# Row factors of the softmax through DRAM into the merge stage, unscaled groups prepared first, normalisation on ScalarE, in a decoder layer of three mixers

## What is computed

```python
def one_block(args):                       # fox_attention, 128 queries of all 8 heads
    scores = jnp.einsum('bqhd,bkhd->bhqk', qi, k) * scale
    logits = jnp.where(mask[None, None], scores + bias, -jnp.inf)
    p = jax.nn.softmax(logits, axis=-1)
    return jnp.einsum('bhqk,bkhd->bqhd', p, v)
...
y_b = fox_attention(...) * jax.nn.silu(gbf)
merged = (gates[:, :, 0] * (y_a @ w_up_a) + gates[:, :, 1] * (y_b @ w_up_b)
          + gates[:, :, 2] * (y_c @ w_up_c))
out = merged @ w_out
return layer_norm(ALPHA * x + out, ln_g, ln_b)
```

## Time and profile before

| | us |
|---|---|
| median of 3 runs | 1954.6 (1950.67 to 1956.67) |
| profiled execution, its own time | 1956.44 |
| its span | 1954.8 |
| PE busy | 1916.7 |
| PEld busy | 1625.1 |
| DVE busy | 1125.0 |
| ACT busy | 708.7 |
| POOL busy | 435.1 |

### The profile page before, as it was taken

One profiled execution on the slowest core, in us unless ns is written; L12 is line 12 of the kernel. 1 busy time (PEld: TensorE's weight loads), 2 busy tenths in 40 slices (PEclk: granted clock), 3 DMA queues, 4 the chain that ended last, 5 costly groups with the idle time before them and its releaser, 6 DMA issues. The chain is left out here.

```text
span 1954.8 us, 30551 instructions
## 1 busy us (share of the span) xinstructions
PE 1916.7 (98%) x10560; PEld 1625.1 (83%) x10560; DVE 1125.0 (58%) x2142; ACT 708.7 (36%) x1090; POOL 435.1 (22%) x548
## 2 busy tenths in 40 slices
PE   7999999999999999999999999999999989999998
PEld 6878887888886888888888788888888878999997
DVE  4563235654244655646556665565655568777676
ACT  3121113021033554555555655455555541111110
POOL 1927940498000000000000000000000002222322
PEclk9999999999999999999999999999999989999999
DMA  6224225322432142241513515133142286555542
GB/s 187 65 91 117 89 86 193 66 97 109 138 120 87 56 124 68 66 125 48 138 54 89 186 50 139 54 89 109 48 136 66 87 262 208 167 174 170 174 118 87
DMA packets 105592, 221.69 MB, mean 113 GB/s; under 512 B 11000, under 2 KB 56744, under 8 KB 101928
## 3 DMA queue, kind: packets, MB, share of 16 engines
q1 hardware_dynamic: 92912, 165.61, 26.8%
q0 software_dynamic: 12608, 55.19, 10.2%
HBM read 155.09 MB, written 65.08 MB: 113 GB/s over the span
## 5 line engine op out<-in xcount | busy, mean ns | idle before, releaser
L1447 PE MATMUL g_ps<-x_hi,w_lo 128*128 128x512 f32 x768 | 309.7, 403 | 0.0
L1447 PE MATMUL g_ps<-x_hi,w_hi 128*128 128x512 f32 x768 | 308.2, 401 | 0.0
L1361 DVE TENSOR_TENSOR pt_lo<-t_ps,pt_hi 128x512 fp32r<-128x512 f32 (+2 forms) x320 | 191.7, 607 | 134.3 <-ACT pt_hi L1269 132.9
L1447 PE MATMUL g_ps<-x_lo,w_hi 128*128 128x512 f32 x768 | 228.1, 412 | 3.7 <-PEq L1484 2.7
L697 PE MATMUL tile_ps<-x_hi,w_hi 128*128 128x512 f32 x736 | 228.4, 391 | 1.5 <-DVE w_lo L379 1.5
L697 PE MATMUL tile_ps<-x_lo,w_hi 128*128 128x512 f32 x736 | 226.7, 389 | 0.0
L697 PE MATMUL tile_ps<-x_hi,w_lo 128*128 128x512 f32 x736 | 226.6, 389 | 0.0
L1269 ACT ACTIVATE pt_hi<-t_ps 128x512 fp32r<-128x512 f32 (+2 forms) x320 | 170.4, 534 | 135.0 <-PE t_ps L1406 130.6
L1177 POOL DMA_DIRECT2D mixT<-y_out x63 | 33.8, 536 | 749.4 <-DVE y_out L1315 749.4
L1301 DVE CUSTOM_DVE_ANT_0 s_sb<-s_ps,f_row 128x512 f32<-128x512 f32 (+2 forms) x320 | 180.7, 605 | 19.5 <-PE s_ps L1395 18.8
L1406 PE MATMUL t_ps<-ident,s_sb 128*128 128x128 f32 x1088 | 171.7, 273 | 1.6 <-DVE pt_lo L1361 1.0
(11 more groups left out here) (294 smaller groups left out, 3576.4 us busy)
## 6 DMA issues: line engine op xcount, KB each, us to landing
w_lo_raw<-in_w_tiles SPq DMA_DIRECT2D x96, 512.0 KB, 3.6
gateT<-g_out SPq DMA_DIRECT2D x96, 256.0 KB, 3.0
gate<-gateT SPq DMA_DIRECT2D x64, 384.0 KB, 4.5
qkvT<-zout SPq DMA_DIRECT2D x24, 512.0 KB, 3.2
x_lo_raw<-in_xT SPq DMA_DIRECT2D x20, 512.0 KB, 8.5
silT<-zout SPq DMA_DIRECT2D x16, 512.0 KB, 2.6
k_ll<-qkvT POOLq DMA_DIRECT2D x16, 512.0 KB, 7.4
q_st<-qkvT POOLq DMA_DIRECT2D x16, 512.0 KB, 9.1
```

What stands on the lines that cost most here:

```text
L1361: dve.tensor_tensor(pt_lo[part], t_ps[n % 2][:, 0:keys].rearrange("p (k q) -> p k q", q=P), pt_hi[part].bitcast(F32), ALU.subtract).then_i ...
L1447: mm = pe.matmul(g_ps[c][:], w[j % 2][:, k, :], x[:, k, c * BANK:(c + 1) * BANK], start=(r == 0), stop=(r == 3 * KT - 1))
```

## The change

Attention no longer divides. `y_out` is stored unscaled to `mixT`. The reciprocals of all 16 tiles are taken at once at the head's last tile, PE transposes them in one 16-column matmul into 16 rows of 128 queries, DVE copies these to `inv_row`, and POOL stores them to a new DRAM scratch `inv` of 128 rows (`store_inv`). The last head does this twice: after its first tiles (two rows are wanted early) and at its end, where SP stores the other 14 rows.

In the merge, SP loads the factors of a block with two DMAs (`load_inv`), each broadcasting rows of four heads to 64 partitions, into the part of `y_lo` that belongs to groups 1 and 2. That is free once the block before has lifted its last step, so SP waits for `lifted` in step d = 6. DVE multiplies `sil` of groups 1 and 2 by the factors (`scale`) ahead of `mix *= sil`. From the second block on, groups 0 and 3 (unscaled) are prepared first, and PE waits for all four groups before the block's first matmul instead of for one after another. For the first block the order of the groups stays.

The normalisation `(x - mean) * rstd` of 128x1024 moves from DVE to ACT as one activation with scale `rstd` and bias `-mean * rstd`; DVE computes the bias in one more small operation. The tail after the last block is as before.

```diff
-            def output(at, p):
+            def output(at, p, last):
                 dve.wait_ge(o_low_ready, at(8, p + 1))
-                dve.wait_ge(y_free, at(8, p + 1))
-                dve.tensor_tensor(y[:], o_ps[0:HD, 0, :], o_low[:], ALU.add).then_inc(o_sum, 1)
-                dve.wait_ge(o_sum, at(8, p + 1))
-                dve.tensor_tensor(y[:], y[:], o_ps[0:HD, 1, :], ALU.mult).then_inc(y_ready, 1)
+                dve.wait_ge(y_free, at(9, p + (2 if last and p >= 3 else 1)))
+                dve.tensor_tensor(y_out[p % 2], o_ps[0:HD, 0, :], o_low[:], ALU.add).then_inc(y_ready, 1)
...
+                if p == 7 or (last and p == 0):
+                    dve.tensor_copy(inv_row, o_ps[0:Q_TILES, 1, 0:P]).then_inc(y_ready, 1)
...
-                    if t % 2 == 1:
+                    if t == Q_TILES - 1 or (last and t == 1):
                         dve.wait_ge(p_ready, at(Q_TILES, t + 1))
-                        dve.reciprocal(row_inv[:, t - 1:t + 1], row_sum[:, t - 1:t + 1]).then_inc(inv_ready, 1)
+                        dve.reciprocal(row_inv[:, 0:t + 1], row_sum[:, 0:t + 1]).then_inc(inv_ready, 1)
...
-                pe.wait_ge(inv_ready, at(8, p + 1))
-                for a in range(2):
-                    last = pe.transpose(o_ps[0:HD, 1, a * P:(a + 1) * P],
-                                        row_inv[:, 2 * p + a:2 * p + a + 1].broadcast_to([P, HD]), ident[:])
-                last.then_inc(o_full, 1)
+                if p == 7 or (final and p == 0):
+                    pe.wait_ge(inv_ready, at(1, 2 if final and p else 1))
+                    mm = pe.transpose(o_ps[0:Q_TILES, 1, 0:P], row_inv[:, 0:Q_TILES], ident[:])
+                mm.then_inc(o_full, 1)
...
+            sp.wait_ge(y_ready, HEADS * 9 + 1)
+            sp.dma_start(scr["inv"][(HEADS - 1) * Q_TILES + 2:], inv_row[2:]).then_inc(last_y_stored, 16)
...
+def load_inv(eng, kept, scr, b):
+    rows = scr["inv"].rearrange("(h t) q -> h (t q)", t=Q_TILES)
+    for odd in range(2):
+        eng.dma_start(kept.y_lo[odd * HD:(odd + 1) * HD, 2:6].bitcast(F32),
+                      rows[odd::2, bass.ds(b * BLOCK, BLOCK)].partition_broadcast(HD)).then_inc(kept.mix_loaded[1], 16)
...
+    def scale(g):
+        dve.wait_ge(kept.mix_loaded[1], b * 64 + 64)
...
+        dve.tensor_tensor(kept.sil[g][:], kept.sil[g][:], group(kept.y_lo, g).bitcast(F32),
+                          ALU.mult).then_inc(kept.scaled, 1)
...
                 for d in range(KT):
+                    if d == KT - 2 and not last:
+                        sp.wait_ge(lifted, b * KT + KT)
+                        load_inv(sp, kept, scr, b + 1)
                     sp.wait_ge(m_split, b * KT + (d + 1))
...
+            def normalise(b, m):
+                act.wait_ge(h_rstd, b * 10 + (5 * m + 5))
+                act.activation(x_t[m][:], x_t[m][:], ACT.Identity, scale=rstd[m][:], bias=fix[m][:]).then_inc(h_norm, 1)
...
-                return dve.tensor_scalar(x_t[m][:], x_t[m][:], mean_var[m][:, 0:1], rstd[m][:], ALU.subtract, ALU.mult)
+                dve.tensor_scalar(t, mean_var[m][:, 0:1], r, -1.0, ALU.mult, ALU.mult).then_inc(h_rstd, 1)
...
-                            if d == 0 and k % (KT // YG) == 0:
-                                pe.wait_ge(y_split, b * YG + (k // (KT // YG) + 1))
+                            if d == 0 and k % (KT // YG) == 0 and (first or k == 0):
+                                pe.wait_ge(y_split, b * YG + (k // (KT // YG) + 1 if first else YG))
```

More of the change, by code:

```diff
@@ L1045, in stage_attend @@
         g_bias = sb("g_bias", [P, T_GATE])
-        g_out, y_out = kept.g_out, kept.y_out
+        g_out, y_out = kept.g_out, [y[0:HD] for y in kept.y_out]
+        inv_row = kept.y_out[0][HD:HD + Q_TILES, 0:P]
         k_hh = sb("k_hh", [P, S], F32R)
@@ L1371, in body @@
                                           kept.wu_hi[:, KT - 1 - i].bitcast(F32), ALU.subtract).then_inc(kept.wu_split, 1)
[L1372 removed]
+                    split_y(dve, kept, 0, True)
                 else:
                     split_kq(at(1, 2))
[L1375 removed]
+                output(at, 7, last)
                 for j in splits("tail", last):
@@ L1506, in group, with split_y, product @@
     return t[:, g * (KT // YG):(g + 1) * (KT // YG)]
-def split_y(dve, kept, b):
+def load_inv(eng, kept, scr, b):
[3 more added lines that the diff above has]
+                      rows[odd::2, bass.ds(b * BLOCK, BLOCK)].partition_broadcast(HD)).then_inc(kept.mix_loaded[1], 16)
+Y_ORDER = (0, 3, 1, 2)
+def split_y(dve, kept, b, first=False):
+    order = range(YG) if first else Y_ORDER
+    def scale(g):
+        dve.wait_ge(kept.mix_loaded[1], b * 64 + 64)
+        if g != 1:
+            dve.wait_ge(kept.mix_loaded[g], b * 32 + 32)
+        dve.tensor_tensor(kept.sil[g][:], kept.sil[g][:], group(kept.y_lo, g).bitcast(F32),
+                          ALU.mult).then_inc(kept.scaled, 1)
+    def product(g):
+        if g in (1, 2):
+            dve.wait_ge(kept.scaled, b * 2 + g)
+        else:
+            dve.wait_ge(kept.mix_loaded[g], b * 32 + 32)
+        dve.tensor_tensor(kept.mix[g][:], kept.mix[g][:], kept.sil[g][:], ALU.mult).then_inc(kept.prod, 1)
     def finish(g):
-        dve.wait_ge(kept.y_high, b * YG + (g + 1))
+        dve.wait_ge(kept.y_high, b * YG + (order.index(g) + 1))
         dve.tensor_tensor(group(kept.y_lo, g), kept.mix[g][:], group(kept.y_hi, g).bitcast(F32),
                           ALU.subtract).then_inc(kept.y_split, 1)
-    for g in range(YG):
-        dve.wait_ge(kept.mix_loaded[g], b * 32 + 32)
-        dve.tensor_tensor(kept.mix[g][:], kept.mix[g][:], kept.sil[g][:], ALU.mult).then_inc(kept.prod, 1)
-        if g:
-            finish(g - 1)
-    finish(YG - 1)
+    if first:
+        product(0)
+        scale(1)
+        scale(2)
+        finish(0)
+        product(1)
+        product(2)
+        finish(1)
+        product(3)
+        finish(2)
+        finish(3)
+    else:
+        product(0)
+        product(3)
+        finish(0)
+        finish(3)
+        scale(1)
+        scale(2)
+        product(1)
+        product(2)
+        finish(1)
+        finish(2)
 def stage_merge(nc, io, scr, kept, out):
@@ L1638, in high_y @@
             def high_y(b):
-                for g in range(YG):
-                    act.wait_ge(prod, b * YG + (g + 1))
+                for n, g in enumerate(Y_ORDER):
+                    act.wait_ge(prod, b * YG + (n + 1))
                     act.activation(group(y_hi, g), mix[g][:], ACT.Copy).then_inc(y_high, 1)
@@ L1650, in body @@
                         root(b - 1, 1)
+                    if not first and d == 5:
+                        normalise(b - 1, 1)
                     act.wait_ge(merged, b * KT + (d + 1))
```

93 lines of the change are left out of this document (53 added, 40 removed).

## The result

The changed kernel takes 1958.2 us (median of 20 runs, 1952.7 to 1963.3) where the kernel before took 1952.6 (20 runs): ratio 1.0023, 95% interval 1.0016 to 1.0030. It is slower by about 0.23% (4.5 us; the medians differ by 5.6), which lies just inside the 0.3% that I took for what can be told from no change; with 20 runs each the interval excludes no change. Forecast: 1946.5, 8.1 us less than before. Its profiled execution took 1959.4 us, span 1957.8 (before 1956.4 and 1954.8).

The account below looks back on a forecast made before the run. TensorE, busy 1916.7 of 1954.8 us, was taken as the bound nearly everywhere. Attention -13.1, its end +0.8, second merge block +4.2 and steady blocks 0 sum to -8.1, so 1946.5 us; range 1941.5 to 1951.

Parts of the forecast that it names:

- Steady blocks, "0 us": Six later merge boundaries: y ready 9.4 us early now, over 8 after the change, so no cost.
- Factors arrive late: Rival, steady merge blocks: late factors stop TensorE at every boundary, 23 us in all, time 1970; chance 0.05.
- ScalarE's activation of 128x1024 lies in its idle time: Steady merge blocks: the normalisation moved to ScalarE is covered there, part of the 0 us.
- Second block, +4.2: Merge, block 1: later landing (1.3), nine operations behind it, TensorE's wait and slow clock; +4.2 us, ends +0.8 to +6.8.
- Attention, -13.1 +0.8 = -12.3: Attention and its end: 119 of 128 factor transposes removed give -13.1 us; later stores at the barrier add 0.8.
- a factor transpose is worth less than its starts say: Rival, attention: removed transposes worth 0.088 us each, so -10.4 instead of -13.1, time 1949.2; chance 0.06.
- attention gives less: Rival, attention: another engine's latency paces some tiles, half of the 13.1 us turns into waits, time 1953.0; chance 0.12.
- VectorE's answer comes earlier by more: Attention, after a pair's values: without the multiplication (0.34 us) VectorE's pt_lo comes earlier by more than TensorE's 0.22.
- End of attention, +0.8: Barrier before the merge: two more products and a second store delay SP and the merge by 0.8 us, ends 0.5 and 1.5.
- Normalisation on ScalarE, at nothing: Merge: VectorE hands 0.81 us of normalisation to ScalarE and gains one small operation; counted as no cost.
- The signs of being wrong: Heads not 1.4 to 1.9 us shorter, idle time at a steady boundary, or block 1's wait under 3 or over 8 us.

Follow-up runs that it names:

- own_rows: The changed kernel with the merge's factor loads of blocks 1 to 7 reading rows of silT instead, same number, size and place; ratio 0.9990 to the kernel before, median 1950.1 us.
- copies8: The change with factors stored 8 times, last store after block 0's fourth gate load, natural group order, normalisation on VectorE; ratio 0.9978 to the kernel before.
- no_loads: The changed kernel without the factor loads of blocks 1 to 7, every other instruction kept; ratio 0.9980 to the kernel before, median 1949.2 us.

## Why the prediction was wrong, point by point

No one term explains the miss. The trace is 11.2 us above the sum's -8.1: attention with its end 5.2, the second block 3.3, the steady blocks 3.7 and the last one 0.4, less 1.4 ahead of the heads. In the steady blocks the mechanism was wrong; elsewhere sizes were.

- **Steady blocks, "0 us": the step that failed.** "VectorE has y ready 9.4 us early" and "the factor loads go out at `lifted` 8 and are wanted some 9 us on" left the landing unpriced; a sil load's 8.8 us would have fitted. The second load took 10.1 to 10.7, and VectorE wanted it 5 us after the first was issued (1750.99 to 1755.99). 37.8 us of VectorE's waits came of it, and 3.7 us on TensorE. own_rows shows the source as the cause: with other rows, the same loads leave 44.6 in every block.
- **The rival that came true, in part.** "Factors arrive late" was given 0.05 and a threshold of 18 us from issue to landing, since only the wait for `y` was costed. That wait never stopped TensorE in steady blocks. What stopped it was the second `gate`, behind two adds that GpSimd's late operations stretched, and that at 10.9 to 11.6 us from the first issue to the last landing (0.3 to 1.3 us a block), while 7.5 to 8.4 (own_rows) and 8.7 to 10.1 (copies8) cost nothing. I had asked who waits for `y`, and not which other engines work later because VectorE waits, and what they then meet. "ScalarE's activation of 128x1024 lies in its idle time" is of the same kind: true of ScalarE, but GpSimd starts when it ends. How much of the 3.7 us the normalisation's new place has was not tested; own_rows and no_loads have it there and lose nothing. The path through GpSimd is read from the traces; no run moved GpSimd's operations alone.
- **Second block, +4.2, measured +7.5.** The mechanism was right: nine operations in 5.8 us, a wait of 5.8 forecast and 7.8 found, clock at 0.50 behind it, no wait at step 2. The term mis-sized is the delay of the last landing: 1.3 by bytes over 355 GB/s, 3.1 measured, above its upper bound of 2.6. own_rows returns 3.9 us of block 0 (no_loads 2.9). The longer wait is 2.0 of the 3.3 us that the forecast lacked. The other 1.3 are in block 1, which gained 0.2 instead of the 1.6 that the sum gave it: its old wait of 1.8 is gone, but the slow stretch costs 2.5 (5 us at 0.50) where the sum had 2.0, and there is a new wait of 0.8 us for the second `gate`, whose adds again meet GpSimd (1.89 and 2.50 us).
- **Attention, -13.1 +0.8 = -12.3, measured -7.1.** The removed transposes gave their 13.1 us, start by start, but the transposes behind them took 1.7 back. That leaves 11.4 us, 0.096 for each of 119: the rival "a factor transpose is worth less than its starts say", with 0.06, came true in part, for 1.7 of its 2.7 us. The rest: the tiles' transposes start 2.2 us later behind the filling work, 1.3 of it the longer waits for `pt_lo` (1.0 to 2.3 us), where VectorE and ScalarE carry the weight split, so the rival "attention gives less", with 0.12, holds in part; the barrier takes 1.2, and 0.9 lies in small pieces. "VectorE's answer comes earlier by more" was wrong at that tile. Moving the split (three runs) moved the wait and gained nothing; no place without a wait was found. Part of the size is scatter: the same attention code takes 947.3 us here, 944.7 in own_rows and 944.5 in no_loads (7.1 to 9.9 less than before), and the old one 952.4 to 954.5. The range had no room for any of this: its worst bound gave attention -12.4, 0.7 from the sum, and names no row for it.
- **End of attention, +0.8.** TensorE's wait at the barrier is 3.9 us instead of 2.6, +1.3: within the ends named.
- **Normalisation on ScalarE, at nothing.** It costs 2.1 us (0.4 to 4.1) alone, 1.5 of it in block 1 by the trace.
- **The signs of being wrong.** Two of the three came. Four of the regular heads are 0.6 to 1.5 us shorter and one is 0.3 longer (not 1.4 to 1.9), and steady blocks show idle time. The third did not: the wait before block 1, 7.8 us, is under 8.

Counting by the trace: -1.4 -7.1 +7.5 +3.7 +0.4 = +3.1 us. The ratio says 4.5 and the medians 5.6, so 1.5 to 2.5 us of the loss aren't in this pair of executions.

## What to carry to other kernels

Price a new transfer by its access pattern and its landing, not by its bytes: rows that many partitions read again are worth storing many times when the store is hidden. Where a wait is added, cost everything that is queued behind it on that engine, and follow the engines fed by it too: here the bound engine was stopped by an add that only became long because a third engine had come late. And put an added transfer where the DMA engines idle: the same 448 KB were dear ahead of block 0's gate loads (56.0 us) and cheap behind four of them (53.6).

## What the hardware showed

- Two loads of 256 KB in which 64 partitions read the same 1 KB rows keep the DMA engines 0.64 to 0.82 busy at 72 to 129 GB/s, and the second lands after 10.1 to 10.7 us; with rows of their own for each partition, windows with the same two loads under way show 264 GB/s and up, and the second lands after 6.7 to 7.6. The Trainium skill, "DMA: Bandwidth & Descriptors", section "Rules for kernel authors", confines a DMA whose outermost dimension has fewer than 16 entries to at most that many engines; here that dimension is 64 in both kernels, so the rule does not tell them apart.
- An add of 128x256 on VectorE takes 0.42 us, and up to 2.50 when GpSimd works on `x_t` beside it; `gate<-gate,u_ps`, which reads PSUM, stays at 0.95.
- Taking out a transpose is worth less than the 0.110 us between its start and the next one: the instructions behind it took back 1.7 of 13.1 us, which leaves 0.096 for each.
